# A mixture-of-experts gate matrix: one-hot products, or softmax weights scattered over zeros in DRAM

## The chip, the cores and the metric

The kernel runs on one core of one Trainium2 chip. The time is device microseconds of one execution. Five engines work side by side and meet at semaphores: TensorE (PE; its weight loads are listed as PEld), VectorE (DVE), ScalarE (ACT), GpSimd (POOL) and SyncE (SP). DMA transfers are issued from the queues of SP, ACT and POOL and share 16 DMA engines.

## The reference

Two transformer blocks on 512 tokens of width 1024. The change lies in the last part of the second block, a PEER layer with 8 heads and 128 x 128 = 16,384 experts:

```python
q = (xb @ w_query).reshape(T, 8, 2, 128)
s = einsum('thpk,hpnk->thpn', q, sub_keys)             # two lists of 128 scores per head
top_s, top_i = top_k(s, 16)
cand_s = top_s[:, :, 0, :, None] + top_s[:, :, 1, None, :]
cand_i = top_i[:, :, 0, :, None] * 128 + top_i[:, :, 1, None, :]
best_s, best_pos = top_k(cand_s.reshape(T, 8, 256), 16)
idx = take_along_axis(cand_i..., best_pos)             # 8 x 16 = 128 experts per token
gate = softmax(best_s)
act = gelu(einsum('td,thkd->thk', xb, expert_u[idx]))
out = einsum('thk,thkd->td', gate * act, expert_v[idx])
```

Each token has 128 picks, 16 in each of 8 heads. Two heads may pick the same expert; their gates then add.

## The kernel before, in words

**Weights in chunks.** Every weight matrix comes as chunks of 512 KB (128 rows of 1024 floats), 462 in all, through a ring of four buffers. SP issues the load (L687), ScalarE rounds to the high half WH (`split_high`, L261), VectorE subtracts for the low half WL (`split_low`, L267), and TensorE multiplies three times, high by high, high by low and low by high (`mm3`, L270 to L274). SP waits for the low half four chunks back, ScalarE for the multiplication four chunks back. So a chunk is split about three chunks ahead of its multiplication, and the three engines follow one order of chunks that is written out by hand.

**The peer_u stage.** 144 chunks, numbered p = 0 to 143: 16 query projections among the first 24, and 128 chunks of peer_u. For each of the latter TensorE makes one 128 x 512 block of x times u (128 experts by 512 tokens), ScalarE applies GELU (L1101) and SP stores it into the DRAM tensor `acts` (expert column, expert row, token). Beside them VectorE finds the picks, one tile of 128 tokens at a time: `pairs` (the best 16 of 256 sums, for two heads a call), `shifted`, `summed` (the numbers of the picks, found by comparing places that POOL subtracts at L795) and `listed` (the softmax). Calls of `low_of_next` stand between them, each one split; the tuples LOWS_LISTED and LOWS_SHIFTED say at which split each part ends, so that ScalarE and TensorE, in their own orders, take part at the same chunk.

**The gate matrix.** Tokens 0 to 383 (three tiles, DW = 384) are done densely: for them the kernel needs the gate of every expert. Before, TensorE transposes the lists of a tile (row number, column number, weight), ScalarE copies them (L1146), and from chunk 80 on 48 groups of 8 tokens follow (`before_gates`). For a group VectorE makes a 128 x 128 one-hot matrix of the row numbers for each token (L1707) and, with POOL's subtraction (L807), one of the column numbers times the weights (L1710); TensorE multiplies them, a float32 product of 128 x 128 per token (L2172, 16 instructions a group); ScalarE copies the result into a staging buffer (L1123) and after 8 groups writes 4 MB to the DRAM tensor `gate_matrices` (L1126).

**The v stage.** 128 chunks of peer_v, v = 0 to 127. For each, `weights(v)` on VectorE multiplies gates by acts (L1719), ScalarE rounds the product (L1135), VectorE makes its low half (L1723), and TensorE adds 18 products of 128 x 512 into PSUM, for three tiles. Gates and acts come in groups of four v, from DRAM, through a ring of two buffers (`load_group`, 768 KB and 768 KB, L1129 and L1130, issued from ScalarE's queue). The load of group j waits until VectorE has used the last weights of group j - 2. Gate reads are runs of 1 KB, act reads of 1.5 KB.

**The last tile.** Tokens 384 to 511 are done by gathering: for each of the 128 picks POOL gathers 128 rows of peer_v by indirect DMA (`pick_row`, L814, six buffers) and 128 acts of four bytes (`pick_acts`, L822), and VectorE adds row times weight into PSUM (`sum_row`, L1739), one per v. POOL starts them when the gate matrices have been written.

Of the kernel before, what the change touches and what calls it, by code (L numbers as in the profile page):

```python
# [13 lines left out]
F32 = mybir.dt.float32  # L14
F32R = mybir.dt.float32r
# [6 lines left out]
P = 128  # L22
# [23 lines left out]
NU = DW // 64  # L46
NG8 = 8 * NU
PICKS = PH * TOPK
SLOTS = 6
# [30 lines left out]
LOWS_LISTED = (47, 59, 71, 77)  # L80
LOWS_SHIFTED = (35, 47, 59, 71)


def before_gates(n):
    return 80 + 3 * n // 4

def constants():  # L90
# [27 lines left out]
    cols["token"] = (GT_TILE * P + i[:, None]).astype(f)  # L118
# [7 lines left out]
    for n, m in enumerate((64, 32, 16, 8, 4, 2, 1)):  # L126
# [7 lines left out]
              ("causal", P), ("cmp_ok", NT * 32), ("cmp_no", NT * 32), ("iota", P), ("four", 4), ("token", 1)]  # L134
# [12 lines left out]
def build(nc, d):  # L147
# [3 lines left out]
    with ExitStack() as ctx:  # L151
# [485 lines left out]
        LST = [A[:, 21504:21888], A[:, 21888:22272], XF[:, 0:384]]  # L637
        LST = [x.rearrange("p (l t) -> p l t", l=3) for x in LST]
        APART = XF[:, 2048:4096].rearrange("p (r i n) -> p r i n", r=2, i=8)
        zg, zs8 = misc(8), misc(8)  # L640

        HALF = 64
        STG = A[:, 0:16384].rearrange("p (r i t) -> p r i t", r=2, i=P)
        OHA = A[:, 16384:18432].rearrange("p (r n) -> p r n", r=16)
        OHB = A[:, 18432:20480].rearrange("p (r n) -> p r n", r=16)

        ACTED = [GATE[:, 0, 0:512], GATE[:, 0, 512:1024], ROW[:, 0:512], ROW[:, 512:1024]]
        G4 = A[:, 0:8 * DW].rearrange("p (r u i t) -> p r u i t", r=2, u=NU, i=4)
        AC = A[:, 8 * DW:16 * DW].rearrange("p (r i t) -> p r i t", r=2, i=4)
        WGHr = over("A", "WGH", 16 * DW, 4 * DW, F32R).rearrange("p (r t) -> p r t", r=4)  # L650
        WGLr = over("A", "WGL", 20 * DW, 4 * DW, F32R).rearrange("p (r t) -> p r t", r=4)
        WGH = WGHr.bitcast(F32)
        WF = A[:, 24 * DW:26 * DW].rearrange("p (r t) -> p r t", r=2)


        ROWS = A[:, 26 * DW:26 * DW + SLOTS * D].rearrange("p (r n) -> p r n", r=SLOTS)
        assert 26 * DW + SLOTS * D <= 16384
# [12 lines left out]
        acts_kept = nc.dram_tensor("acts", (P, P, S), F32, kind="Internal").ap()  # L670
        act_list = acts_kept.rearrange("e p (t o) -> (e p t) o", o=1)
# [75 lines left out]
        def _(pool):  # L747
# [35 lines left out]
            pool.dma_start(ROW[:, :], dr["nf_post"].partition_broadcast(P)).then_inc(sem("row_landed"), 16)  # L783
            pool.wait_ge(sem("rows_weighted"), 2 * NT)
# [5 lines left out]
            def places_apart(t, i):  # L790

                wait(pool, "eq_summed", 4 * t + i)
                p3 = PAB.rearrange("p s u -> p (s u)")[:, i * 64:i * 64 + 64].rearrange("p (h k) -> p h k", k=TOPK).unsqueeze(3)
                it = con("iota")[:, 0:TOPK].unsqueeze(1).unsqueeze(1)
                nc.gpsimd.tensor_tensor(EQ, p3.to_broadcast([P, PH // 2, TOPK, TOPK]),  # L795
                                        it.to_broadcast([P, PH // 2, TOPK, TOPK]), ALU.subtract).then_inc(sem("eq_ready"), 1)

            for t in range(NT):
                pool.wait_ge(sem("places_ready"), t + 1)
                for i in range(4):  # L800
                    places_apart(t, i)
            pool.wait_ge(sem("list_stored"), ND)
            pool.wait_ge(sem("picks_listed"), 1)
            for n in range(NG8):
                wait(pool, "onehot_ready", n - 1)
                nums = LST[n // 16][:, 1, 8 * (n % 16):8 * (n % 16) + 8].unsqueeze(2).to_broadcast([P, 8, P])
# [19 lines left out]
            for r in range(2):  # L826
                pool.wait_ge(sem(f"gates_written{r}"), 16 * NU // 2)
# [16 lines left out]
        def _(act):  # L844
# [268 lines left out]
            gm = dr["gate_matrices"]  # L1113

            def store_gates(n):
                u = n // 8
                if n % 8 == 0:
                    wait(act, f"gates_written{u % 2}", 16 * (u // 2))
                for b in (2 * n, 2 * n + 1):
                    act.wait_ge(sem("gm_ready"), b + 1)  # L1120
                    at = 4 * (b % 16)
                    dst = STG[:, u % 2].rearrange("p i t -> p t i")[:, at:at + 4, :]
                    nc.scalar.activation(dst, PS[:, b % 4, :].rearrange("p (t n) -> p t n", t=4), ACT.Copy)                        .then_inc(sem("gm_stored"), 1)  # L1123
                if n % 8 == 7:
                    act.wait_ge(sem("gm_stored"), 16 * (u + 1))
                    act.dma_start(gm[u], STG[:, u % 2]).then_inc(sem(f"gates_written{u % 2}"), 16)  # L1126
# [10 lines left out]
            for p in range(24, QU):  # L1137
                high_of_next()
                gelu(u_of(p))
                for t in range(NT):  # L1140
# [3 lines left out]
                    if t < ND and p == LOWS_LISTED[t] - 2:  # L1144
                        act.wait_ge(sem("list_turned"), t + 1)
                        nc.scalar.activation(LST[t], PS[:, 4, 0:3 * P].rearrange("p (l t) -> p l t", l=3), ACT.Copy)                            .then_inc(sem("list_stored"), 1)  # L1146
# [1127 lines left out]
```

## Time and profile before

| | us |
|---|---|
| median of 3 runs | 2643.19 (2641.51 to 2643.9) |
| the profiled execution | 2637.98 |
| its span on the core | 2636.1 |
| PE busy | 2519.1 (96%) |
| DVE busy | 1579.1 (60%) |
| ACT busy | 1027.7 (39%) |
| POOL busy | 502.8 (19%) |

Rows are read so. A group by line: line, engine, operation, out <- in with shapes, count | busy us, mean ns of one | idle time of the engine just before them, and what ended most of it. A window: its bounds and length, then busy us and count of PE, PEld, DVE, ACT and POOL, the granted clock of TensorE (1 is the full 2.4 GHz), the mean busy share of the DMA engines, GB/s. A timeline: start us, duration us, engine, line, operation, and in brackets the idle time before it. A piece of the chain: start, length, what. Matmuls are pipelined, so one of 0.39 us starts every 0.2267 us in a full stretch. A busy share of the DMA engines can come out slightly above 1.

### The profile page before, as it was taken

Reading aid. Unit: us, or ns where it says so; the run is one execution under the profiler, and the core shown is the slowest. Engines: PE = TensorE matmul, PEld = TensorE weight load, DVE = VectorE, ACT = ScalarE, POOL = GpSimd, SP = SyncE. Lnnn points to the kernel's source line nnn. Section 1 sums busy time; section 2 is a strip of 40 time slices with the busy share of each in tenths; the row PEclk is TensorE's granted clock in tenths of the full one; section 3 lists DMA queues with packets and bytes.
Section 4 is the critical chain, followed back from the end, with each engine's and each line's share of the span. In section 5 each row is a group of like instructions: output and inputs, shape, how many; then the busy total and the mean of one; then the engine's idle time right before and its main releaser. Section 6 shows DMA issues by size and latency. Waiting matters only on the chain.

```text
span 2636.1 us, 31762 instructions
## 1 busy us (share of the span) xinstructions
PE 2519.1 (96%) x11982; PEld 2081.6 (79%) x11982; DVE 1579.1 (60%) x2604; ACT 1027.7 (39%) x1452; POOL 502.8 (19%) x363
## 2 busy tenths in 40 slices
PE   7999998999999999899999999999999999899995
PEld 6876676888888788778888888888888778777784
DVE  4365665555543577467767755556322777777777
ACT  4353443433332644543333334555422333333332
POOL 0030000000000000000011123333100755566651
PEclk9997999999999999999999999999999999999998
DMA  6223343233322222133344443546645899889994
GB/s 207 82 67 97 94 137 99 85 98 99 97 96 96 80 80 72 57 117 104 122 146 144 144 144 139 205 160 229 236 146 190 308 329 334 310 320 320 316 336 145
DMA packets 162696, 434.03 MB, mean 165 GB/s; under 512 B 17072, under 2 KB 59072, under 8 KB 161280
## 3 DMA queue, kind: packets, MB, share of 16 engines
q1 hardware_dynamic: 94896, 276.96, 31.6%
q10 hardware_dynamic: 43424, 77.60, 8.4%
q0 software_dynamic: 24240, 77.63, 7.9%
q8 instruction: 89, 1.46, 0.2%
q14 instruction: 47, 0.39, 0.0%
HBM read 369.21 MB, written 62.91 MB: 164 GB/s over the span
## 4 chain that ended last, share of the span: by engine, by line
PE 71%; DVE 11%; DMA 8%; issue 4%; ACT 4%; POOL 1%; ACTq 0%; DVEq 0%; SPq 0%; POOLq 0%
PE PS L272 20%; PE PS L274 20%; PE PS L273 20%; DVE WL L267 4%; DMA A<-acts 4%; DMA A<-gate_matrices 3%; DVE PS L1739 3%; PE PS L2172 3%; DVE A L1719 2%; ACT WGH L1135 1%; PE PS L1935 1%; PE PS L2072 1%; PE PS L2019 1%; PE PS L2006 1%; POOL A L822 1%
## 5 line engine op out<-in xcount | busy, mean ns | idle before, releaser
L267 DVE TENSOR_TENSOR WL<-RAW,WH 128x1024 fp32r<-128x1024 f32 x462 | 587.1, 1272 | 557.9 <-ACT WH L261 520.6
L272 PE MATMUL PS<-HH,WH 128*128 128x512 f32 x1696 | 667.4, 394 | 8.8 <-DVE HL L433 7.1
L273 PE MATMUL PS<-HL,WH 128*128 128x512 f32 x1696 | 660.8, 390 | 0.0
L274 PE MATMUL PS<-HH,WL 128*128 128x512 f32 x1696 | 660.8, 390 | 0.0
L261 ACT ACTIVATE WH<-RAW 128x1024 fp32r<-128x1024 f32 x462 | 485.2, 1051 | 247.5 <-PE PS L274 209.6
L272 PEld LDWEIGHTS PS<-HH,WH 128*128 128x128 f32 x1696 | 318.8, 188 | 79.2 <-DVE HL L433 10.3
L274 PEld LDWEIGHTS PS<-HH,WL 128*128 128x128 f32 x1696 | 318.6, 188 | 66.6
L273 PEld LDWEIGHTS PS<-HL,WH 128*128 128x128 f32 x1696 | 318.9, 188 | 63.4
L272 PE MATMUL PS<-WH,WGH 128*128 128x512 f32 x768 | 307.2, 400 | 39.4 <-DVE WGL L1723 38.6
L273 PE MATMUL PS<-WL,WGH 128*128 128x512 f32 x768 | 304.8, 397 | 0.0
L274 PE MATMUL PS<-WH,WGL 128*128 128x512 f32 x768 | 304.4, 396 | 0.0
L814 POOL DMA_INDIRECT A<-in_peer_v,V_AT x128 | 187.9, 1468 | 225.7 <-DVE PS L1739 176.9
L272 PEld LDWEIGHTS PS<-WH,WGH 128*128 128x128 f32 x768 | 148.1, 193 | 75.4 <-issue 43.3
L1135 ACT ACTIVATE WGH<-A 128x384 fp32r<-128x384 f32 x128 | 67.2, 525 | 335.6 <-DVE A L1719 333.9
L273 PEld LDWEIGHTS PS<-WL,WGH 128*128 128x128 f32 x768 | 148.4, 193 | 30.9
L274 PEld LDWEIGHTS PS<-WH,WGL 128*128 128x128 f32 x768 | 147.8, 192 | 31.5
L1739 DVE SCALAR_TENSOR_TENSOR PS<-A,PS 128x1024 f32<-128x1024 f32 x127 | 163.0, 1283 | 2.1 <-DVE A L1732 0.6
L822 POOL DMA_INDIRECT A<-acts,A_AT x128 | 147.2, 1150 | 48.9 <-issue 38.7
L272 PE MATMUL PS<-WH,HH 128*128 128x512 f32 (+1 forms) x352 | 137.5, 391 | 12.5 <-DVE A L1554 5.5
L273 PE MATMUL PS<-WL,HH 128*128 128x512 f32 (+1 forms) x352 | 136.0, 386 | 0.0
L274 PE MATMUL PS<-WH,HL 128*128 128x512 f32 (+1 forms) x352 | 136.0, 386 | 0.0
L1101 ACT ACTIVATE ROW<-PS 128x512 f32<-128x512 f32 x64 | 38.3, 598 | 235.7 <-PE PS L274 235.7
(338 smaller groups left out, 3077.8 us busy)
## 6 DMA issues: line engine op xcount, KB each, us to landing
RAW<-in_peer_u SPq DMA_DIRECT2D x128, 512.0 KB, 3.5
RAW<-in_peer_v SPq DMA_DIRECT2D x128, 512.0 KB, 7.0
RAW<-in_w_ada SPq DMA_DIRECT2D x48, 512.0 KB, 3.7
gate_matrices<-A ACTq DMA_DIRECT2D x6, 4096.0 KB, 12.6
A<-gate_matrices ACTq DMA_DIRECT2D x32, 768.0 KB, 7.9
A<-acts ACTq DMA_DIRECT2D x32, 768.0 KB, 13.0
RAW<-in_ffn_up SPq DMA_DIRECT2D x44, 512.0 KB, 3.4
acts<-GATE SPq DMA_DIRECT2D x64, 256.0 KB, 2.3
```

Of the source, the lines that this page charges most:

```text
L261: nc.scalar.activation(WHr[:, slot(c), 0:w], RAW[:, slot(c), 0:w], ACT.Copy).then_inc(sem("high_done"), 1)
L267: nc.vector.tensor_tensor(WLr[:, slot(c), 0:w], RAW[:, slot(c), 0:w], WH[:, slot(c), 0:w], ALU.subtract).then_inc(sem("low_done"), 1)
L272: nc.tensor.matmul(out, L[0], R[0], start=first, stop=False)
L273: nc.tensor.matmul(out, L[0], R[1], start=False, stop=False)
L274: return nc.tensor.matmul(out, L[1], R[0], start=False, stop=last)
L814: pool.indirect_dma_start(out=ROWS[:, u % SLOTS, :], out_offset=None, in_=dr["peer_v"], in_offset=bass.IndirectOffsetOnAxis(ap=V_AT[:, u:u ...
L822: pool.indirect_dma_start(out=AG[:, u:u + 1], out_offset=None, in_=act_list, in_offset=bass.IndirectOffsetOnAxis(ap=A_AT[:, u:u + 1], axis ...
L1101: nc.scalar.activation(ACTED[k % 4], PS[:, 5 + k % 3, :], ACT.Gelu).then_inc(sem("gelu_done"), 1)
L1135: nc.scalar.activation(WGHr[:, v % 4, :], WF[:, v % 2, :], ACT.Copy).then_inc(sem("w_high"), 1)
L1719: nc.vector.tensor_tensor(WF[:, v % 2, :].rearrange("p (u t) -> p u t", u=NU), AC[:, j % 2, v % 4, :].rearrange("p (u t) -> p u t", u=NU), ...
L1739: ins = nc.vector.scalar_tensor_tensor(ACC, row, PW[:, u:u + 1], ACC, ALU.mult, ALU.add)
L2172: last = nc.tensor.matmul(PS[:, b % 4, j * P:(j + 1) * P], OHA[:, r, :], OHB[:, r, :], start=True, stop=True)
```

## The change

- The one-hot products go: POOL's subtractions, VectorE's two one-hot matrices a group, TensorE's products, the transposes of the lists, ScalarE's copies and the six writes of 4 MB.
- A DRAM tensor `gates` (129 x 128 x 384 floats: expert column, expert row, token) takes their place. POOL fills its first 128 slabs with zeros in 16 DMAs of 1.57 MB, one per two chunks of the up projection of the first block. VectorE waits for them before it overwrites the zeros' source, in the win2 stage.
- For each of the three dense tiles VectorE makes two lists of 128 numbers per token. `apart` compares each head's 16 experts with those of all heads before it, and sends a pick that came before to slab 128, which is never read. `merged` makes, for each pick, the sum of the weights of all picks with the same expert (128 instructions over 128 elements with an accumulated output). After every 16 a semaphore lets POOL go on.
- POOL scatters them: 3 x 128 indirect DMAs, each of which writes 128 floats, one per token.
- `summed` compares places itself on VectorE. `listed` of tile t is followed by `apart` and `merged` of tile t, no longer interleaved with the pairs of the next one. The splits stand at other places (LOWS_SHIFTED 35, 58, 81, 104).
- ScalarE waits at chunk 138 (QU - 6) for all scatters, where it waited for the writes of the gate matrices.
- The gate and act rings have three buffers in place of two, the row ring seven in place of six. The load of group j is issued at v = 4j - 11 (it was 4j - 6), when group j - 3 is used up. Gate reads are runs of 1.5 KB.
- POOL's first row picks wait for the picks' list and stand behind the scatters.

```diff
-SLOTS = 6
+SLOTS = 7
+GROUPS = 3
-LOWS_LISTED = (47, 59, 71, 77)
-LOWS_SHIFTED = (35, 47, 59, 71)
+LOWS_SHIFTED = (35, 58, 81, 104)
...
@@ POOL
+            nc.gpsimd.memset(ZERO, 0.0).then_inc(sem("zero_set"), 1)
+            for n in range(16):
+                pool.wait_ge(sem("chunk_used"), FIRST["up"] + 2 * n + 1)
+                pool.dma_start(gates_kept.rearrange("e p t -> p e t")[:, 8 * n:8 * n + 8, :],
+                               ZERO.unsqueeze(1).to_broadcast([P, 8, DW])).then_inc(sem("gates_zeroed"), 16)
...
-            for n in range(NG8):
-                nc.gpsimd.tensor_tensor(APART[:, n % 2], con("iota").unsqueeze(1).to_broadcast([P, 8, P]), nums,
-                                        ALU.subtract).then_inc(sem("rows_apart"), 1)
+            for t in range(ND):
+                for u in range(PICKS):
+                    if u % 16 == 0:
+                        pool.wait_ge(sem("picks_merged"), PH * t + u // 16 + 1)
+                    pool.indirect_dma_start(out=gate_list, out_offset=bass.IndirectOffsetOnAxis(ap=PLACE[:, t, u:u + 1], axis=0),
+                                            in_=MERGED[:, t, u:u + 1], in_offset=None).then_inc(sem(f"gates_placed{t}"), 16)
...
-            for r in range(2):
-                pool.wait_ge(sem(f"gates_written{r}"), 16 * NU // 2)
+            pool.wait_ge(sem("picks_listed"), 1)
             for u in range(SLOTS):
                 pick_row(u)
@@ ScalarE
                 if p == QU - 6:
-                    for r in range(2):
-                        act.wait_ge(sem(f"gates_written{r}"), 16 * NU // 2)
+                    for t in range(ND):
+                        act.wait_ge(sem(f"gates_placed{t}"), 16 * PICKS)
...
-                    for j in range(2):
+                    for j in range(GROUPS):
                         load_group(j)
...
-                if v % 4 == 2 and 2 <= v // 4 + 2 < P // 4:
+                if v % 4 == 1 and v // 4 + GROUPS < P // 4:
@@ VectorE
+            def apart(t):
+                places = []
+                nc.vector.memset(TIMES[:, 0:TOPK], 0.0)
+                for h in range(1, PH):
...
+                    done = mark(nc.vector.tensor_tensor(same, EXPERT[:, hs].unsqueeze(2).to_broadcast([P, TOPK, n]),
+                                                        EXPERT[:, 0:n].unsqueeze(1).to_broadcast([P, TOPK, n]), ALU.is_equal))
+                    until(done)
+                    places.append(mark(nc.vector.tensor_reduce(TIMES[:, hs], same, AX, ALU.add)))
+                    low_of_next(h in (3, 5, 7))
...
+            def merged(t, b):
+                for u in range(16 * b, 16 * b + 16):
+                    last = nc.vector.scalar_tensor_tensor(SAME[:, u % 16, :], EXPERT, EXPERT[:, u:u + 1], GW, ALU.is_equal,
+                                                          ALU.mult, accum_out=MERGED[:, t, u:u + 1])
+                last.then_inc(sem("picks_merged"), 1)
+                dve.wait_ge(sem("picks_merged"), PH * t + b + 1)
...
+            for t in range(NT):
                 for i in range(4):
                     low_of_next()
+                    last = pairs(t, i)
+                    low_of_next()
+                until(last)
+                shifted(t)
+                for i in range(4):
+                    low_of_next()
+                    summed(t, i)
+                listed(t)
+                if t < ND:
+                    apart(t)
+                    for b in range(PH):
                         low_of_next()
+                        merged(t, b)
@@ TensorE
-            def gates_of(n):
-                pe.wait_ge(sem("onehot_ready"), n + 1)
-                for b in (2 * n, 2 * n + 1):
-                    wait(pe, "gm_stored", b - 3)
-                    for j in range(4):
-                        r = 8 * (n % 2) + 4 * (b % 2) + j
-                        last = nc.tensor.matmul(PS[:, b % 4, j * P:(j + 1) * P], OHA[:, r, :], OHB[:, r, :],
-                                                start=True, stop=True)
-                    last.then_inc(sem("gm_ready"), 1)
```

## Rows read from the trace of the kernel before

**Rows 1.** The page, busy time of the engines

```profile
PE 2519.1 (96%) x11982; PEld 2081.6 (79%) x11982; DVE 1579.1 (60%) x2604; ACT 1027.7 (39%) x1452; POOL 502.8 (19%) x363
```

**Rows 2.** Windows: up projection; one-hot products; v stage; two short stretches of it

```profile
510.00:760.00 250.00, 250.00 (x1105) 207.01 (x1104) 138.24 (x163) 89.45 (x119) 0.00 (x0) 1.00 0.30 97
1604.00:1883.00 279.00, 279.00 (x1603) 244.75 (x1603) 161.11 (x127) 145.24 (x167) 89.47 (x44) 1.00 0.49 182
...
2035.00:2616.00 581.00, 541.48 (x2304) 442.98 (x2304) 435.56 (x524) 193.98 (x255) 329.75 (x252) 0.96 0.88 309
...
2200.00:2210.00 10.00, 10.00 (x46) 8.29 (x45) 5.39 (x6) 1.97 (x3) 5.63 (x5) 1.00 1.04 398
...
2282.00:2286.00 4.00, 1.25 (x3) 1.09 (x4) 2.32 (x3) 1.51 (x2) 2.87 (x3) 0.51 0.27 62
```

**Rows 3.** Groups by line, of TensorE, VectorE and POOL in the v stage

```profile
L272 PE MATMUL PS<-WH,WGH 128*128 128x512 f32 x768 | 307.2, 400 | 39.4 <-DVE WGL L1723 38.6 <-ACT ROW L1101 0.7
...
L1719 DVE TENSOR_TENSOR A<-A 128x384 f32<-128x384 f32 x128 | 70.7, 552 | 54.3 <-issue 46.1 <-DMA A<-acts 8.1
...
L822 POOL DMA_INDIRECT A<-acts,A_AT x128 | 147.2, 1150 | 48.9 <-issue 38.7
```

**Rows 4.** ScalarE's timeline: GELU of chunks 24, 25 and 143

```profile
1299.92 0.60 ACT L1101 ACTIVATE GATE<-PS 128x512 f32<-128x512 f32 x1 [4.88 <-PE PS L274]
...
1305.36 0.60 ACT L1101 ACTIVATE GATE<-PS 128x512 f32<-128x512 f32 x1 [3.89 <-PE PS L274]
...
2034.61 0.60 ACT L1101 ACTIVATE ROW<-PS 128x512 f32<-128x512 f32 x1 [3.48 <-PE PS L274]
```

**Rows 5.** The chain, first and last of the twelve long pieces of L2172

```profile
1600.18 3.57 PE PS L2172 x32
...
1858.75 3.57 PE PS L2172 x32
```

**Rows 6.** DMA issues: KB each, us to landing; the act loads' own view

```profile
RAW<-in_ffn_up SPq DMA_DIRECT2D x44, 512.0 KB, 3.4
...
L1130 ACTq DMA_DIRECT2D A<-acts x32: 567/568/1710, 2008.0 to 2575.4; - x32
...
DMA to landing us min/median/max: 6.6/13.0/23.8
```

**Rows 7.** VectorE's timeline: a call of `pairs`, a split, `summed`, part of `listed`

```profile
1389.68 0.75 DVE L1620 TENSOR_TENSOR X<-X 128x256 f32<-128x256 f32 x2
...
1394.04 1.20 DVE L267 TENSOR_TENSOR WL<-RAW,WH 128x1024 fp32r<-128x1024 f32 x1
1395.16 1.42 DVE L1646 SCALAR_TENSOR_TENSOR A<-A,X 128x256 f32<-128x256 f32 x4
1396.62 1.22 DVE L1649 TENSOR_REDUCE X<-A 128x64 f32<-128x1024 f32 x1
...
1401.12 0.29 DVE L1659 TENSOR_TENSOR X<-X,MISC 128x128 f32<-128x128 f32 x1
```

**Rows 8.** Groups by line: ScalarE's reads of its accumulator

```profile
L921 ACT ACTIVATION_READ_ACCUMULATOR A<-PS,MISC 128x1 f32 x64 | 12.4, 194 | 0.0
```

**Rows 9.** Timelines of POOL and VectorE in the v stage; landing times of L822

```profile
2137.00 0.95 POOL L822 DMA_INDIRECT A<-acts,A_AT  x1 [0.30 <-issue]
...
2143.02 1.28 DVE L1739 SCALAR_TENSOR_TENSOR PS<-A,PS 128x1024 f32<-128x1024 f32 x1
...
2143.26 0.95 POOL L822 DMA_INDIRECT A<-acts,A_AT  x1 [0.30 <-issue]
...
2049.42 0.56 DVE L1723 TENSOR_TENSOR WGL<-A,WGH 128x384 fp32r<-128x384 f32 x1 [0.59 <-ACT WGH L1135]
2049.50 1.30 POOL L822 DMA_INDIRECT A<-acts,A_AT  x1 [0.30 <-issue]
...
2440.01 1.68 POOL L814 DMA_INDIRECT A<-in_peer_v,V_AT  x1 [2.26 <-DVE PS L1739]
...
DMA to landing us min/median/max: 2.3/5.0/8.1
```

More of the change, by code:

```diff
@@ new lines, in build @@
+        WGH = WGHr.bitcast(F32)
+        WF = A[:, o4 + 2 * GD:o4 + 2 * GD + 2 * DW].rearrange("p (r t) -> p r t", r=2)
+        o5 = o4 + 2 * GD + 2 * DW
+        ROWS = A[:, o5:o5 + SLOTS * D].rearrange("p (r n) -> p r n", r=SLOTS)
+        SAME = A[:, o5:o5 + 2048].rearrange("p (r n) -> p r n", r=16)
+        SAME2 = A[:, o5 + 2048:o5 + 4096].rearrange("p (r n) -> p r n", r=16)
+        TIMES, PLACED = A[:, 21248:21376], A[:, 21376:21504]
+        assert 11264 <= o5 and o5 + SLOTS * D <= 20480
@@ L658, in build @@
+        PLACE = over("A", "PLACE", 21504, ND * PICKS, U32).rearrange("p (t u) -> p t u", t=ND)
+        MERGED = A[:, 21888:22272].rearrange("p (t u) -> p t u", t=ND)
+        ZERO = A[:, 21504:21504 + DW]
         ACC = PS[:, 2 * GT_TILE:2 * GT_TILE + 2, :]
@@ L1641, in summed @@
             def summed(t, i):
-                dve.wait_ge(sem("eq_ready"), 4 * t + i + 1)
+                places = PAB.rearrange("p s u -> p (s u)")[:, i * 64:i * 64 + 64].rearrange("p (h k) -> p h k", k=TOPK)
+                ranks = con("iota")[:, 0:TOPK].unsqueeze(1).unsqueeze(1)
+                link(nc.vector.tensor_tensor(EQ, places.unsqueeze(3).to_broadcast([P, PH // 2, TOPK, TOPK]),
+                                             ranks.to_broadcast([P, PH // 2, TOPK, TOPK]), ALU.is_equal))
@@ L1644, in summed @@
                 for h in range(PH // 2):
                     num = TFf[:, i * 64 + 16 * h:i * 64 + 16 * h + TOPK].unsqueeze(1).to_broadcast([P, TOPK, TOPK])
[L1646 to L1650 removed]
+                    last = nc.vector.tensor_tensor(EQ[:, h], EQ[:, h], num, ALU.mult)
@@ L2178, in _ @@
                 acts(u_of(p))
-                for t in range(NT):
-                    if t < ND and p == LOWS_LISTED[t] - 2:
-                        pe.wait_ge(sem("list_ready"), t + 1)
-                        wait(pe, "list_stored", t)
-                        for l, src in enumerate((N12[:, t % 2, 0], N12[:, t % 2, 1], BV[:, t % 2].rearrange("p h k -> p (h k)"))):
-                            last = nc.tensor.transpose(PS[:, 4, l * P:(l + 1) * P], src, ident)
-                        last.then_inc(sem("list_turned"), 1)
-                for n in range(NG8):
-                    if before_gates(n) == p + 1:
-                        gates_of(n)
             pe.wait_ge(sem("gelu_done"), P)
```

154 lines of the change are left out of this document (46 added, 108 removed).

## The prediction

> **What bounds the kernel now.** I read the page first. TensorE is busy for 96% of the span [rows 1], so the first question of every edit is whether it takes TensorE work away or makes TensorE wait. Then the windows by stage, which show three states [rows 2]. In the up projection and in the stage with the one-hot products TensorE is busy all the time at granted clock 1.00. In the last stage (the 128 chunks of peer_v, here "the v stage") it is busy 541.5 of 581 us at clock 0.96, and the DMA share is 0.88. Third, the groups by line [rows 3]: in the v stage TensorE sat idle 39.4 us, nearly all of it behind the weights L1723, and VectorE 54.3 us before L1719, the line that waits for the gate and act groups. Fourth, ScalarE's timeline in the peer_u stage, which gives the pace: one chunk per 5.44 us, with the GELU of chunk 24 ending at 1300.5 and that of the last, chunk 143, at 2035.2 [rows 4]. 119 chunks x 5.44 would end at 1947.9, so 87.3 us is something else. The chain shows what: twelve pieces of 32 instructions of L2172, the one-hot products, of 3.57 us each [rows 5]. They are half of its 768, the rest stands in shorter pieces between; 24 x 3.57 = 85.7 us. Three sets of transposes make up the rest. TensorE never waits there for anything but its own work.
>
> **The change, part by part.**
> *One-hot products and transposes out.* They are wholly on TensorE's path: -87.3 us. The ScalarE copies, the six 4 MB writes, POOL's subtractions and VectorE's one-hot rows that fed them ran beside TensorE and give nothing themselves.
>
> *Zeros.* 16 writes of 1.57 MB (25.2 MB) over some 32 chunks of the up stage add about 145 GB/s to 97 [rows 2]; the same table has 398 GB/s in one stretch. A weight chunk lands in 3.4 us [rows 6] and is asked for about two chunks (10.9 us) ahead; one zero block at 398 GB/s is 4.0 us, so even right behind one it comes at 7.4 us. Cost 0; if that cover fails, up to 16 x 4 us.
>
> *VectorE's new list work.* A tile now has 23 chunks, 23 x 5.44 = 125 us. In it: 23 splits at 1.2 = 28; four pairs of searches at 4.35 (1389.68 to 1394.04 [rows 7]) = 17; the place comparison (about 1.2), four products (1.42) and the sum (1.22) four times = 15; the comparisons of `apart`, 7,168 elements and as many summed, at 1.22 us per 1,024 elements = 17; small steps 4; and 128 instructions of `merged`. Their duration is not in the trace. Lower bound: the pitch of a 128-wide operation, 0.21 us (0.29 long [rows 7], of which some 0.08 overlaps the next). Upper: that plus 0.19, what ScalarE's accumulator read takes [rows 8]. So 27 to 51 us, 108 to 132 in all for 125. I take 0.29 (37 us): VectorE keeps up. At the upper end it is late by 7 us per tile against a lead of nearly three chunks, about 10 us of waits at most, and those lie ahead of the wait below and come off it. Price 0.
>
> *The scatter, on POOL.* 384 indirect DMAs in a row, and nothing else passes it: the row picks queue behind it. The nearest rows are L822's gathers, 128 four-byte elements each [rows 3, 9]. With VectorE idle one takes 0.95 us plus 0.30 between (2137.0), also beside an operation with one of its inputs in PSUM (2143.3); one that starts inside an operation with two inputs in SBUF waits for its end and takes 1.30 (2049.5). The mean over the v stage is 1.15 + 0.30 = 1.45. Here the splits occupy 1.2 of 5.44 us: 0.22 x half of 1.2 = 0.13 us each; the list work by the same sum adds 0.14. So 1.53 us while VectorE builds lists, 1.39 later. Start: split L becomes possible some 1 us (the high half) after the GELU of chunk L - 4, at 1301.5 + 5.44 (L - 28) [rows 4]; the first `merged` block stands behind split 42, 1377.7, and the long comparisons before it put it some 11 us behind: 1389. VectorE's lists end near split 108, 1737: 348 us, 228 scatters. The other 156 take 217 us: 1954, and 5.0 us to land [rows 9]: 1959.
> ScalarE asks for all of them after the GELU of chunk 138, at 1920.7, and nothing passes it. Queued behind: the first group loads and the high halves of chunks 142 and on. TensorE can go on to the end of 141 (1937). Restart: six issues at up to 0.57 [rows 6], 3 us, high and low half 2.3, chunks 142 and 143 10.9: the v stage begins at 1975 in place of 1947.9. After a gap TensorE also runs slowly at first: granted clock 0.51, the lower level of 1.2 GHz, in 2282 to 2286 [rows 2], when it had just stood idle. All gaps of the v stage cost 541.5 - 522 = 19 us that way, about 2 each. Together +29. Bounds: 1.26 us per scatter, no wait, 0; 1.68 + 0.30 as L814 after a wait [rows 9], the slow rival below.
> The SBUF — State Buffer page of the Trainium skill ("Who interferes with whom") says of `tensor_tensor` that it was not seen to stall DMA, since descriptor generation needs the write side only. The trace differs here: 1.30 against 0.95 beside exactly such an operation. By that rule each scatter would be 1.26 us and the wait would be nothing.
>
> *Deeper rings, longer gate rows.* 2,304 matmuls at 5.44/24 = 0.2267 us are 522 us, the stage, whose window [rows 2] holds them all, lasts 580: 58 us of late groups and slow restarts. A group is asked for when its buffer is free, four v before its use, 16 us, and the act loads take 6.6 to 23.8 us to land [rows 6]. With three buffers the lead is eight v, 33 us, more than the longest. What is late next is DMA itself: share 0.88 x 580/522 = 0.98, rate 309 x 580/522 = 343 GB/s, against 1.04 and 398 in a full stretch [rows 2]. That leaves few per cent, so not all comes back. Gate reads of 1.5 KB runs in place of 1 KB help a little. Bounds 0 and 58; I take 46, nearer the upper since the longest landing fits. A seventh row buffer: 0, rows aren't waited for now. The end after the last matmul is as before.
>
> **Sum** against the profiled execution, 2638.0: -87.3 +29 -46 = 2533.7. The median of the runs shown is 5.2 us over that execution, so 2539.
>
> **Rivals.**
> 1. *The scatter hides.* At up to about 1.37 us each it is done by 1915 and landed by 1920: 2510. For: 0.95 + 0.30 whenever VectorE is idle. Against: the 1.45 mean. 20%.
> 2. *The DMA engines are the bound of the v stage.* The groups still come late, since 0.98 of share is no reserve, and the 46 stay out: 2585. For: full stretches already occur. Against: there are nearly idle ones too, around each stall (share 0.27 in 2282 to 2286 [rows 2]). 20%.
> 3. *Slower: a scatter costs more than a gather.* Place: POOL, between chunk 39 and the wait at 138. Each 0.1 us over 1.53 moves the end by 38 us one for one. All gains are gone when the v stage begins at 2035 + 46 = 2081, that is (2081 - 21 - 1389)/384 = 1.75 us each. At 1.98, L814's rate after a wait, scatters end at 2149, the v stage starts at 2171 and the time is about 2734. For: no row shows a four-byte write to DRAM; an engine's eight writes may not overlap. Against: the gathers of the same shape do. 12%.
> The DMA: Bandwidth & Descriptors page of the Trainium skill (Specifications) speaks for it: under 512 bytes a transfer becomes a read-modify-write. No run here shows that yet.
> 4. *The lists make VectorE late*, `merged` at over 0.4 us: TensorE waits in each of three tiles, and the wait at 138 shrinks by as much; some 2550. 5%.
> The rest, 43%, is the forecast. The change does take the products out, so a change that does nothing is not a rival.
>
> **How the numbers follow.** 2539 is the likeliest case. The low end, 2495, is rival 1 with the whole 58 us; the high end, 2610, lies past rival 2 and holds scatters up to about 1.63 us with the 46 regained. Left out are most of rival 3 and a mix of 1 with more. A measurement of this kernel tells about 0.2%, 5 us, from no change. Faster: the forecast, rivals 1, 2 and 4, less 2 for places where two go wrong together = 0.86. Of those 2 and rival 3's 12, 11 are slower and 3 the same.
>
> **What would show it.** Right: no L2172; GELU every 5.44 us up to chunk 138; then one gap of TensorE of 20 to 35 us whose releaser is the landing of a scatter; POOL busy without a break from about 1390 to 1950, 1.4 to 1.5 us per scatter; in the v stage VectorE's idle time before `weights` at a fifth of 54 us and DMA share 0.95 or more. Wrong: a gap over 100 us (rival 3), none (1), a v stage still near 580 us (2), or TensorE waiting for low halves between chunks 39 and 100 (4).

## The result: 2896 us, slower by 9.3%, and the profile after

| | before | after |
|---|---|---|
| median of the runs | 2643.6 us (4 runs) | 2895.6 us (4 runs) |
| ratio, 95% interval | | 1.0932 (1.0882 to 1.0983) |
| profiled execution, span | 2638.0, 2636.1 | 2898.4, 2896.4 |
| last GELU ends | 2035.2 [rows 4] | 2348.6 |
| v stage | about 580 [rows 2] | 527 |

One of the four executions after, 2926.8 us, ran in the chip's slower state and is left out of the ratio.

The forecast was 2539 us and faster. The page of the changed kernel: busy time, the granted clock and the DMA share in 40 slices, the chain by engine, and four groups.

```profile
PE 2495.2 (86%) x11205; PEld 2005.5 (69%) x11205; DVE 1638.4 (57%) x3352; ACT 939.7 (32%) x1353; POOL 769.9 (27%) x700
...
PEclk9997999999999999999757955985599999999998
DMA  5322432664322213234203410330154479999994
...
PE 82%; issue 12%; DVE 3%; ACT 2%; DMA 1%; POOL 0%; DVEq 0%; SPq 0%; ACTq 0%
...
L264 PE MATMUL PS<-HH,WH 128*128 128x512 f32 x1696 | 681.6, 402 | 108.8 <-issue 99.1
...
L796 POOL DMA_INDIRECT gates<-A,PLACE x384 | 391.1, 1019 | 547.6 <-DVE A L1662 412.1
...
L1662 DVE SCALAR_TENSOR_TENSOR A<-A 128x128 f32<-128x128 f32 x384 | 114.4, 349 | 71.0 <-issue 70.7
```

TensorE has 777 matmuls fewer than before [rows 1] and yet ends later. The clock falls three times in the middle, the DMA share with it, and 12% of the chain is "issue": time in which an engine waits for nothing that the profile shows. The scatter itself is cheap for POOL: 1.02 us each. The three falls begin some 20 us after POOL starts a burst of scatters; the windows below show them.

The windows of the changed kernel (columns: stretch, its length, then for PE, PEld, DVE, ACT and POOL the busy us with the count of instructions, the granted clock, the DMA share and GB/s): three stretches in which scatters are issued, one between them without scatters, the v stage.

```profile
1388.00:1540.00 152.00, 56.59 (x159) 34.26 (x158) 44.99 (x231) 7.72 (x10) 112.50 (x112) 0.59 0.14 35
...
1640.00:1810.00 170.00, 64.53 (x176) 39.28 (x175) 48.05 (x244) 9.26 (x12) 127.88 (x128) 0.58 0.13 36
...
1904.00:2064.00 160.00, 69.09 (x189) 42.33 (x188) 48.72 (x251) 10.81 (x14) 121.31 (x119) 0.61 0.15 43
...
1574.00:1636.00 62.00, 62.00 (x275) 51.33 (x274) 53.84 (x101) 21.04 (x27) 0.00 (x0) 1.00 0.41 131
...
2349.00:2876.00 527.00, 523.01 (x2304) 431.83 (x2302) 438.56 (x524) 198.84 (x254) 327.16 (x250) 1.00 0.93 337
```

Without scatters TensorE runs 275 matmuls in 62 us, 4.44 per us. In the first three rows it ran 524 in 482 us; at 4.44 per us they take 118, so 364 us were lost there. What that looks like from inside, in the timeline of all engines (start, duration, engine, instruction, and the idle time before it):

```profile
1449.77 0.97 POOL L796 DMA_INDIRECT gates<-A,PLACE  x1 [0.31 <-issue]
1449.79 0.58 PE L265 MATMUL PS<-HL,WH 128*128 128x512 f32 x1 [2.22 <-issue]
1451.04 0.97 POOL L796 DMA_INDIRECT gates<-A,PLACE  x1 [0.30 <-issue]
1451.18 0.29 PEld L266 LDWEIGHTS PS<-HH,WL 128*128 128x128 f32 x1 [2.51 <-issue]
...
1452.58 0.59 PE L266 MATMUL PS<-HH,WL 128*128 128x512 f32 x1 [2.20 <-issue]
...
1453.98 0.29 PEld L264 LDWEIGHTS PS<-HH,WH 128*128 128x128 f32 x1 [2.51 <-issue]
...
1455.37 0.35 DVE L1662 SCALAR_TENSOR_TENSOR A<-A 128x128 f32<-128x128 f32 x1 [1.31 <-issue]
```

A matmul, a weight load, a matmul, a weight load start at 1449.79, 1451.18, 1452.58 and 1453.98: one instruction of TensorE every 1.40 us, none of which waits for a semaphore. VectorE has such gaps too, if less evenly: most of its instructions in `merged` start 1.40 us apart between 1455 and 1473, but four of them in the same stretch came at their usual 0.27 (1452.34 to 1453.15). POOL keeps its pace of 0.97 + 0.30. The low clock is not the cause: the matmul takes 0.58 us at it, in place of 0.39, but the next starts 2.8 us later. And the DMA engines are not full: their share is 0.14. SP issued 5 weight loads in the 140 us from 1400, where 26 go in a kernel that is not held.

The harm has an onset. These are windows before it, at it and behind it (the count of POOL is that of the scatters):

```profile
1380.00:1400.00 20.00, 20.00 (x90) 16.57 (x89) 19.79 (x106) 5.14 (x7) 9.24 (x9) 1.00 0.56 159
1400.00:1420.00 20.00, 16.25 (x59) 10.84 (x58) 11.74 (x66) 1.96 (x3) 15.62 (x15) 0.90 0.30 80
...
1460.00:1480.00 20.00, 4.11 (x7) 2.00 (x7) 3.17 (x15) 1.54 (x2) 15.42 (x16) 0.50 0.06 14
```

Up to 1410 TensorE runs at full pace beside the scatters. Its first gap comes when 16 of them have started, while the clock is still high; in the other two bursts it comes after about as many. Behind the onset TensorE runs 7 matmuls in 20 us in place of 90. The end of the third burst shows the same with VectorE idle (9 matmuls from 2050 to 2076), so its lists need not run beside the scatters to keep TensorE slow.

The v stage went nearly as forecast: its DMA share is 0.93, where 0.95 or more was expected, and VectorE's idle time before `weights` is gone. The group of L264 there has 4.7 us of idle time in place of 39.4 [rows 3]:

```profile
L264 PE MATMUL PS<-WH,WGH 128*128 128x512 f32 x768 | 299.2, 390 | 4.7 <-DVE WGL L1705 4.0 <-ACT ROW L1088 0.7
```

### The profile page after: what moved, and what is told of

Its sections match the earlier page's. It is cut to its first block, busy times and chain, and to the rows that moved or that the text cites. A ratio compares the mean times of both kernels' runs of the same rounds, so it can differ in the third digit from the quotient of the medians.

```text
span 2896.4 us, 31168 instructions
## 1 busy us (share of the span) xinstructions
PE 2495.2 (86%) x11205; PEld 2005.5 (69%) x11205; DVE 1638.4 (57%) x3352; ACT 939.7 (32%) x1353; POOL 769.9 (27%) x700
## 4 chain that ended last, share of the span: by engine, by line
PE 82%; issue 12%; DVE 3%; ACT 2%; DMA 1%; POOL 0%; DVEq 0%; SPq 0%; ACTq 0%
PE PS L264 25%; PE PS L266 24%; PE PS L265 24%; PE PS L1913 1%; PE PS L2050 1%; PE PS L1997 1%; PE PS L1984 1%; DVE WL L259 1%; PE PS L408 1%; PE PS L2128 0%; PE PS L414 0%; DMA RAW<-in_w_in 0%; ACT WH L253 0%; ACT A L444 0%; PE PS L1916 0%
## 5 line engine op out<-in xcount | busy, mean ns | idle before, releaser
L259 DVE TENSOR_TENSOR WL<-RAW,WH 128x1024 fp32r<-128x1024 f32 x462 | 564.4, 1222 | 712.0 <-ACT WH L253 611.7
L264 PE MATMUL PS<-HH,WH 128*128 128x512 f32 x1696 | 681.6, 402 | 108.8 <-issue 99.1
L265 PE MATMUL PS<-HL,WH 128*128 128x512 f32 x1696 | 677.8, 400 | 110.0 <-issue 109.4
L266 PE MATMUL PS<-HH,WL 128*128 128x512 f32 x1696 | 678.1, 400 | 108.9 <-issue 108.2
L796 POOL DMA_INDIRECT gates<-A,PLACE x384 | 391.1, 1019 | 547.6 <-DVE A L1662 412.1
L264 PEld LDWEIGHTS PS<-HH,WH 128*128 128x128 f32 x1696 | 327.1, 193 | 200.8 <-issue 127.2
L266 PEld LDWEIGHTS PS<-HH,WL 128*128 128x128 f32 x1696 | 327.0, 193 | 200.7 <-issue 136.8
L265 PEld LDWEIGHTS PS<-HL,WH 128*128 128x128 f32 x1696 | 327.3, 193 | 189.8 <-issue 127.5
L264 PE MATMUL PS<-WH,WGH 128*128 128x512 f32 x768 | 299.2, 390 | 4.7 <-DVE WGL L1705 4.0
L1088 ACT ACTIVATE GATE<-PS 128x512 f32<-128x512 f32 x64 | 38.3, 598 | 455.0 <-PE PS L266 215.2
L264 PEld LDWEIGHTS PS<-WH,WGH 128*128 128x128 f32 x768 | 144.1, 188 | 36.1 <-issue 5.2
L1662 DVE SCALAR_TENSOR_TENSOR A<-A 128x128 f32<-128x128 f32 x384 | 114.4, 349 | 71.0 <-issue 70.7
L264 PE MATMUL PS<-WH,HH 128*128 128x512 f32 (+1 forms) x352 | 137.6, 391 | 12.6 <-DVE A L1524 5.5
```

What stands on the lines that cost most here:

```text
L259: nc.vector.tensor_tensor(WLr[:, slot(c), 0:w], RAW[:, slot(c), 0:w], WH[:, slot(c), 0:w], ALU.subtract).then_inc(sem("low_done"), 1)
L264: nc.tensor.matmul(out, L[0], R[0], start=first, stop=False)
L265: nc.tensor.matmul(out, L[0], R[1], start=False, stop=False)
L266: return nc.tensor.matmul(out, L[1], R[0], start=False, stop=last)
L796: pool.indirect_dma_start(out=gate_list, out_offset=bass.IndirectOffsetOnAxis(ap=PLACE[:, t, u:u + 1], axis=0), in_=MERGED[:, t, u:u + 1], ...
L1088: nc.scalar.activation(ACTED[k % 4], PS[:, 5 + k % 3, :], ACT.Gelu).then_inc(sem("gelu_done"), 1)
```

## The experiments

Each starts from the changed kernel unless its diff says otherwise. Where no ratio stands, the time is that of one execution.

### The scatters away, and the deeper rings alone

```diff
# e1: no scatter, no wait for it
-  pool.indirect_dma_start(out=gate_list, out_offset=...PLACE[:, t, u:u + 1]..., in_=MERGED[:, t, u:u + 1], ...)
-  for t in range(ND):
-      act.wait_ge(sem(f"gates_placed{t}"), 16 * PICKS)
# e4: the kernel before, with
-SLOTS = 6
+SLOTS = 7
+GROUPS = 3      # G4 and AC have GROUPS buffers, the loads run GROUPS groups ahead
```

> The changed kernel without its 384 scatters and without ScalarE's wait for them; the merged weights are computed and thrown away, the gate matrix in DRAM stays zero. In the changed kernel the GELU chunks kept a pitch of 5.44 us outside three stretches and 16 to 67 us in them, some 400 us more than their number by 5.44. Theory A (those stretches belong to the scatters, nothing else of the change costs anything): 2897 less 400 is 2497 us; between 2485 and 2515, TensorE's clock above 0.95 from 1388 to 1950 us, last GELU near 1950 us. Theory B (the longer lists of VectorE, or the splits of the gates put ahead, hold TensorE in these stretches): 2800 to 2900 us, the stretches remain.

> The kernel before with the deeper rings alone (three groups of gates and activations on one semaphore each, seven row slots), one-hot products kept. Theory A (the rings are worth the 54 us that the v stage of the changed kernel got shorter, 526 against 580 us): 2643 less 50 is about 2593 us, between 2583 and 2605. Rival (the shorter v stage belongs to what the change removed, not to the rings): 2635 to 2645 us.

Measured: e1 2501.5 us (ratio to before 0.9466, 0.9439 to 0.9494), e4 2588.7 us (0.9801, 0.9779 to 0.9822). Their windows, e1's first burst stretch and v stage, then e4's v stage:

```profile
1380.00:1560.00 180.00, 180.00 (x795) 149.07 (x794) 169.01 (x685) 53.92 (x69) 0.00 (x0) 1.00 0.47 144
...
1950.00:2476.00 526.00, 521.69 (x2298) 431.23 (x2299) 438.10 (x524) 199.17 (x254) 329.80 (x251) 1.00 0.93 337
```

```profile
2038.00:2564.00 526.00, 520.90 (x2289) 430.35 (x2288) 434.94 (x521) 195.34 (x251) 331.15 (x250) 1.00 0.94 336
```

VectorE does all its list work in e1 and TensorE never stops in the stretch: the lists are innocent. The rings are worth 2641.7 - 2588.7 = 53 us (2641.7 is the kernel before, measured beside them), and what the change adds to them without the scatter is worth 2588.7 - 2501.5 = 87.2 us. The loss belongs to the scatters.

### Which property of a scatter does it

Twelve kernels vary three quantities: how many bytes each of the 128 writes has, how far apart they go, and whether in order; the direction (e2) and the kind of transfer (f4) come beside them. The edits, in the line that makes the places and in the transfer:

```diff
-  nc.vector.scalar_tensor_tensor(PLACE[:, t], PLACED, float(DW), token, ALU.mult, ALU.add)
+  # in floats, u the pick, p the partition, t the tile, n1 the first key of the pick
+  # f1: 16384 t + 128 u + p               f2, e3, f3: 128 (16384 t + 128 u + p)
+  # g1, h1, i2: 49152 p + 384 u + 128 t   h2: 49152 u + 384 p + 128 t
+  # g2: 384 (128 u + n1) + 128 t + p      h3: 128 (16384 t + 128 u + n1) + p
# e2: a gather from the changed kernel's own places (slab 128 is zeroed too; the third tile waits for the first)
-  pool.indirect_dma_start(out=gate_list, out_offset=..., in_=MERGED[:, t, u:u + 1], in_offset=None)
+  pool.indirect_dma_start(out=SINK[:, ...], out_offset=None, in_=gate_list, in_offset=...)
# e3, h1: rows of 512 bytes; f3, i2: of 64 bytes
+  pool.indirect_dma_start(out=row_list, out_offset=..., in_=con("mean")[:, 0:128 or 0:16], in_offset=None)
# f4: an ordinary transfer
+  pool.dma_start(gates_kept[u, :, P * t:P * t + 1], MERGED[:, t, u:u + 1])
```

> Every scatter becomes an indirect gather of 128 x 4 bytes from the very same addresses of the gate matrix into a buffer that nobody reads; the matrix stays zero, and one more row of it is zeroed. As many instructions on GpSimd, as many descriptors, the other direction. Theory W (it is the 4-byte writes to DRAM that slow the other engines): about 2497 to 2520 us, no stretch in which TensorE's instructions come 1.4 us apart. Theory I (it is the dense run of indirect transfers with their descriptors, whichever way the data goes): about 2900 us, the three stretches as before.

> Every scatter writes 128 rows of 512 bytes (a constant of the program in place of the weights) to 128 neighbouring rows of the gate matrix, in order; the output is not the reference's. As many transfers and descriptors, 128 times the bytes (25 MB in all, at 1.28 us for 64 KB some 51 GB/s while they run). Theory W with the size as its cause (writes under 512 bytes cost a read as well): the slow stretches are gone, 2500 to 2560 us. Theory I (the run of indirect transfers): stretches as before, 2880 to 3000 us.

> The changed kernel's scatters, 4 bytes from each partition as before, but to 128 neighbouring floats of DRAM (512 bytes in all) in place of 128 far apart ones; the places are now in order, so the output is not the reference's. Theory S (the number of 4-byte writes counts, wherever they go): three slow stretches as in the changed kernel, 2880 to 2900 us. Theory R (it is the far addresses, each write opening another part of the memory): 2525 us like the run with 512-byte rows. Between them, if neighbours collide in one 512-byte line and each must wait for the other: longer than the changed kernel.

> The same 4-byte scatters at a pitch of 512 bytes, in order: the first 4 bytes of each of the rows that the run with 512-byte rows wrote whole; the output is not the reference's. This and that run differ in the size of the write alone. Theory S (small size): 2880 to 2900 us with the three stretches. Theory R (addresses without order): 2525 us.

> The same addresses at a pitch of 512 bytes, each row 64 bytes long (a constant in place of the weights). Theory S as a threshold at 512 bytes (each shorter write costs a read and a write back): 2880 to 2900 us. Rival (only writes shorter than some smaller piece are slow): 2525 us.

> 384 ordinary transfers from GpSimd in place of the indirect ones, each 4 bytes from each partition to fixed places 1536 bytes apart; the output is not the reference's. Theory S (the 4-byte writes, whoever makes their descriptors): the three stretches stay, 2860 to 2950 us. Rival (small writes and indirect descriptors only together, for instance through the writing of the list of places by GpSimd): about 2525 us.

| run | each write | places of one scatter | us | 1400 to 1540: matmuls, clock, DMA share |
|---|---|---|---|---|
| e2 | gather, 4 bytes | the changed kernel's own | 2525.1 | 620, 1.00, 0.47 |
| e3 | 512 bytes | 64 KB in order | 2527.1 | 620, 1.00, 0.60 |
| f3 | 64 bytes | 64 KB in order | 2526.8 | 619, 1.00, 0.49 |
| f2 | 4 bytes | 64 KB in order | 2530.1 | 619, 1.00, 0.48 |
| f1 | 4 bytes | 512 bytes in order | 2566.9 | 611, 1.00, 0.91 |
| f4 | 4 bytes, ordinary | 192 KB in order | 2498.1 | 619, 1.00, 0.51 |

Each of these times stands on one execution. The faster kernels that were executed four times spread over 5 to 12 us (e4, i1, e1), so differences under some 12 us between rows are not read here.

So it is not the run of indirect transfers (e2, e3), and my theory S, that the small size is enough, fell with f2, f3 and f4: none of them holds the engines. f1 shows a different cost. The windows of f2 and then f1:

```profile
1400.00:1540.00 140.00, 140.00 (x619) 115.95 (x619) 129.77 (x497) 43.10 (x55) 110.42 (x98) 1.00 0.48 146
```

```profile
1400.00:1540.00 140.00, 138.48 (x611) 114.35 (x610) 125.40 (x470) 42.52 (x52) 110.72 (x97) 1.00 0.91 133
...
RAW<-in_peer_u SPq DMA_DIRECT2D x25, 512.0 KB, 17.5
```

With 128 neighbouring floats the DMA engines are busy for 0.91 of the time at 133 GB/s and a 512 KB weight load takes 17.5 us to land, but TensorE goes on. It costs 37 us more than f2. Of f4 one thing more: it started 39 transfers of 4-byte writes in the 20 us from 1400, where the change started 15, and TensorE kept its pace. The places remained:

> Every scatter writes its 128 x 4 bytes 192 KB apart, one in each of 128 equal parts of the matrix, in order; the next scatter writes 1536 bytes further on. The output is not the reference's. At a pitch of 512 bytes (64 KB in one scatter) there was no slow stretch; the changed kernel's own places lie anywhere in 25 MB. Theory F (what costs is how far the 4-byte writes of one scatter lie apart): the three stretches are back, 2800 to 2950 us. Theory U (what costs is that the places have no order): about 2530 us.

> The places keep the drawn first key of each pick and lose the second: the 128 x 4 bytes of scatter u lie without order, at 128 rows of 1536 bytes drawn by the picks, in a window of 192 KB that moves on with u; the output is not the reference's. Theory F (distance): no slow stretch, about 2530 us. Theory U (no order): the stretches as in the changed kernel, 2880 us or more.

> The run with 4 bytes every 192 KB (2901 us) with whole 512-byte rows at the same starts, a constant in place of the weights; 25 MB are written. Theory D (many distant places in one scatter are slow, whatever the size): 2850 to 2950 us and the three stretches. Theory M (distance and small size together: a short write to a distant place): 2525 to 2540 us as with 512-byte rows in order.

> Indirect scatters of 4 bytes at a pitch of 1540 bytes in order, 192 KB in each scatter: the window of the run with drawn first keys (2915 us), without its disorder and without two writes in one row; and about the places of the ordinary transfers (2498 us) by indirect ones. Theory O (within 192 KB disorder or rows hit twice are what costs): 2525 to 2535 us. Theory D (a scatter that leaves 64 KB is slow, if its places come by a list): 2880 to 2920 us.

> Indirect scatters of 4 bytes within 64 KB, as in the run with a pitch of 512 bytes in order (2530 us), but each in the row of 512 bytes that the first key of its pick draws: disorder, and rows hit by several partitions. Theory O (disorder or rows hit twice): 2880 us or more. Theory D (distance, pages of 64 KB or the like): 2530 us.

> Rows of 64 bytes, a constant in place of the weights, at the 192 KB pitch at which 4 bytes took 2901 us and 512 bytes 2527. Theory M512 (every write under 512 bytes to a distant place is slow): 2880 to 2920 us. Rival (64 bytes are whole pieces for the memory; only smaller writes are slow): 2527 us.

| run | each write | places of one scatter | us | 1400 to 1540: matmuls, clock, DMA share |
|---|---|---|---|---|
| g1 | 4 bytes | 192 KB apart, in order | 2901.2 | 136, 0.59, 0.12 |
| i2 | 64 bytes | 192 KB apart, in order | 2529.7 | 619, 1.00, 0.50 |
| h1 | 512 bytes | 192 KB apart, in order | 2527.2 | 619, 1.00, 0.60 |
| g2 | 4 bytes | within 192 KB, rows drawn | 2914.9 | 134, 0.57, 0.13 |
| h2 | 4 bytes | within 192 KB, in order | 2531.9 | 620, 1.00, 0.49 |
| h3 | 4 bytes | within 64 KB, rows drawn | 2530.4 | 619, 1.00, 0.48 |

The windows of g1 and h1, which differ in the size of the write alone:

```profile
1400.00:1540.00 140.00, 51.90 (x136) 29.84 (x135) 39.72 (x194) 6.18 (x8) 107.00 (x107) 0.59 0.12 34
```

```profile
1400.00:1540.00 140.00, 140.00 (x619) 115.95 (x618) 129.71 (x491) 42.44 (x55) 110.41 (x98) 1.00 0.60 190
```

Both conditions are needed: 4-byte writes, and places that are scattered widely. Either alone is harmless: 64 and 512 bytes at the widest pitch (i2, h1), 4 bytes within 64 KB or in order within 192 KB (f2, h3, h2). The longer writes were tried in order only, not at drawn places. Theory M had h1 right; its strict form, with a limit at 512 bytes, fell with i2. Theories O and D were each half right: disorder costs in 192 KB and not in 64 KB, distance costs in order too (g1). In g2 and h3 several writes of a scatter can also fall into one row; g2 doesn't tell that from disorder. What unit of distance stands behind this (64 KB is the widest that was harmless without order) is not settled. The places of h2 are 1536 bytes apart by its edit (its expectation says 1540), the same as those of f4. The changed kernel meets both conditions, as its picks are drawn from 16,384 experts in 25 MB.

### How many in flight

```diff
   pool.indirect_dma_start(... MERGED[:, t, u:u + 1] ...)
+  # g3, h4, i1, j1: wait until all but 0, 1, 2 or 3 of the scatters so far have landed
+  # (a semaphore for each scatter in flight)
```

> GpSimd waits for each scatter to land before it makes the next, at most one in flight; all places are the changed kernel's own. Landing takes 2 to 3 us in a quiet stretch, so a scatter each 3.5 to 5 us in place of 1.28. Theory Q (what holds the engines is a queue of unfinished writes, which the rate builds up: the first 12 scatters cost nothing): no slow stretch; but GpSimd needs 384 x 4 = 1540 us, ends near 2930 us, the v stage waits for it, some 3450 us. Rival (each scatter costs the other engines a fixed time, about 1.06 us of TensorE each, whatever the rate): TensorE's clock stays low from 1388 us on, and its instructions are spread out through the whole stretch.

> The changed kernel's own places, at most two scatters in flight. One at a time took 2.87 us for each from 1393 to 2496 us and showed no slow stretch in its first 140 us. With two, 1.6 to 2.0 us for each. Theory Q (a queue that fills above some rate, between one scatter per 1.28 us and one per 2.9 us, and holds the engines only when full): no stretch of slow engines, the scatters end between 2110 and 2180 us, the v stage starts then: 2660 to 2760 us. Rival (each scatter has a fixed price for the engines, which one at a time pays as well): the price per scatter is that of the changed kernel, 1.06 us, and TensorE's clock is low through the stretches, 2900 us.

> The changed kernel with its own places, at most three scatters in flight; the output is whole. Two in flight took 2.39 us for each in the first burst, landing 3.7 us, 1.87 in the second and 1.28 in the third, and held no engine; unlimited scatters that cost nothing (rows of 512 bytes) came every 1.50, 1.47 and 1.37 us and ended at 1944. Theory Q (a queue of unfinished short writes fills only above a number in flight): three in flight give some 1.65, 1.5 and 1.37 us each, the last near 1975, the v stage starts some 30 us later than with 512-byte rows: 2545 to 2580 us, which would beat both kernels. Rival (the rate decides, and near 1.5 us for each the queue fills as before): slow stretches return, TensorE's clock under 0.9 in them, 2750 to 2900 us.

> As with three in flight (2563 us, last scatter at 1979), with at most four; the output is whole. Theory Q (a limit by the number in flight, above four): scatters come at the pace of those that cost nothing (1.50, 1.47, 1.37 us), the last near 1950, 2530 to 2550 us. Rival (the limit lies between three and four, or the rate decides): the slow stretches are back at least in part, over 2600 us, TensorE's clock below 0.95 in 1400 to 1540.

| at most in flight | us | last scatter starts | 1.40 us stretches |
|---|---|---|---|
| 1 (g3) | 3078.5 | 2496.3 | none |
| 2 (h4) | 2685.4 | 2102.5 | none |
| 3 (i1) | 2563.3, ratio to before 0.9721 (0.9675 to 0.9767) | 1978.8 | none |
| 4 (j1) | 2901.3, ratio 1.0964 (1.0928 to 1.0999) | 2078.8 | all three |
| no limit (the change) | 2895.6 | 2075.0 | all three |

The windows of i1, then of j1:

```profile
1388.00:1540.00 152.00, 152.00 (x672) 125.91 (x671) 141.56 (x562) 46.19 (x59) 104.81 (x90) 1.00 0.48 146
...
1640.00:1810.00 170.00, 170.00 (x752) 140.85 (x751) 103.95 (x360) 52.01 (x67) 118.69 (x111) 1.00 0.48 152
```

```profile
1388.00:1540.00 152.00, 64.17 (x201) 43.41 (x200) 55.09 (x266) 12.36 (x16) 105.59 (x106) 0.62 0.17 46
...
1640.00:1810.00 170.00, 62.66 (x179) 38.81 (x177) 52.80 (x263) 10.01 (x13) 120.32 (x120) 0.59 0.14 40
```

Three are harmless, four are as bad as no limit. The waits of POOL say how small the step is; i1, then j1 (waited for: us in total, times, longest):

```profile
POOL gates L796 <- issue: 94.2, 296, 2.2
POOL gates L796 <- DMA gates<-A,PLACE: 79.1, 87, 2.8
```

```profile
POOL gates L796 <- issue: 115.1, 377, 0.4
...
POOL gates L796 <- DMA gates<-A,PLACE: 0.5, 1, 0.5
```

With three allowed POOL was stopped 87 times, 79 us in all. With four it was stopped once, for 0.5 us; so at this pace, which is the change's own, more than four are hardly ever in flight as the semaphores count it, and the change's slow stretches don't need more. So my picture of a long queue that fills (theory Q) fails as a count of scatters that have not landed: between harmless and ruinous lies one more. Something builds up all the same, since the first 16 to 19 scatters of a burst cost nothing in the change, in g1, in g2 and in j1. Whether that is writes for which the semaphore has already been raised, no run here shows.

The limit also lowers the rate, and the two were not varied apart: beside VectorE's lists i1 starts a scatter per 1.69 and 1.53 us (90 in 152 us, 111 in 170), j1 one per 1.43 and 1.42. That the rate decides alone is unlikely, though. From 1826 to 1900 i1 started 53 in 74 us, one per 1.40, and TensorE ran 328 matmuls there, as many as in the same window of the change, where no scatter was under way; j1 fell into its first slow stretch after 16 that came 1.38 us apart. In i1's timeline of POOL in that window the pitch is for most scatters the change's own 1.28 us:

```profile
1850.83 0.97 POOL L796 DMA_INDIRECT gates<-A,PLACE  x1 [0.30 <-issue]
1852.11 0.97 POOL L796 DMA_INDIRECT gates<-A,PLACE  x1 [0.30 <-issue]
1853.50 0.97 POOL L796 DMA_INDIRECT gates<-A,PLACE  x1 [0.43 <-DMA gates<-A,PLACE]
```

i1 is the fastest kernel that computes the whole output. One semaphore wait in POOL's loop turns 2896 into 2563 us. What it still pays is the end of the scatters: the last start of h1 is 1944.2, of i1 1978.8, and those 34.6 us are nearly all of the 36 us between 2527.2 and 2563.3.

## Why the prediction was wrong

**One-hot products out -87.3, zeros 0, VectorE's lists 0: right together.** e1 differs from e4 in all three, and takes 87.2 us less. They weren't measured one by one, so a gain and a loss among them could cancel. `merged` takes 0.35 us with 0.08 for its read beside it, at a pitch of 0.27 where nothing disturbs it; I had taken 0.29.

**Deeper rings, -46: right, a little small.** -53 by e4, and the v stage is 526 us. What I held back, that a share of 0.98 leaves no reserve, wasn't needed: e4 and e1 ran the stage at a DMA share of 0.93 and 0.94 and the clock at 1.00. Rival 2 is out.

**The scatter's own path, +29: right in its total where the writes are harmless, and partly by luck.** In e3 it is 2527.1 - 2501.5 = 25.6, with one gap of 27.2 us, forecast at 20 to 35, and the last GELU ends at 1977.3, forecast 1975. But two terms were off and cancel. The scatters start at 1390.9 and 1944.1, first and last, 1.44 us each, where I had 1.53 and 1.39; the last is out 10 us early, and ScalarE goes on at 1946.5, not 1959. Then its six group loads take 14.3 us to issue, where I had 3: the last alone holds ScalarE for 10.67 us (3.31 us in e1). e3's source view of the scatter, then rows of its timelines of ScalarE and TensorE:

```profile
L797 POOL DMA_INDIRECT gates<-CON,PLACE x384: 965/972/3762, 1390.9 to 1944.1; - x192
...
1946.46 0.40 ACTq L1103 DMA_DIRECT2D A<-gates  x1
...
1950.10 10.67 ACTq L1105 DMA_DIRECT2D A<-acts  x1
...
1963.33 0.76 PE L264 MATMUL PS<-HH,WH 128*128 128x512 f32 x1 [27.20 <-DVE WL L259]
...
1976.65 0.60 ACT L1089 ACTIVATE ROW<-PS 128x512 f32<-128x512 f32 x1 [3.48 <-PE PS L266]
```

The forecast's own terms against the median of before measured beside e1, 2641.7 - 87.3 - 46 + 29, give 2537; the kernels with the same number of harmless indirect transfers (f1 aside) take 2525 to 2532.

**The step that failed.** It is "the nearest rows are L822's gathers", from which the scatter was priced as time of POOL and of the wait at chunk 138 alone. A bound was kept for a dearer scatter (rival 3, 1.98 us each, 2734), but on POOL's account. The real price is on everybody else's: POOL paid 1.02 + 0.30 us per scatter, less than forecast, while TensorE, from some 20 us after the start of each burst to its end, got one instruction per 1.40 us, and VectorE 99 in the 120 us from 1420, where i1 has 374. That is 2898 - 2527 = 371 us against the harmless scatters of e3. So rival 3 had the sign and the missing row ("no row shows a four-byte write to DRAM") and the wrong mechanism: its gap at 138 is not there, and the gap's reason, late scatters, isn't either: the last scatter starts at 2075.0, the first group load behind chunk 138 at 2321.1. The gathers of the same shape and the same addresses (e2) prove nothing about scatters.

**Two slips in the forecast's arithmetic**, which decide nothing: its mean was (1954 - 1389)/384 = 1.47 us per scatter, so rival 3's "each 0.1 us over 1.53" holds over 1.47; and rival 1 with the whole 58 us gives 2498, not 2495.

**The rule of the Trainium skill** that I set beside rival 3 (DMA: Bandwidth & Descriptors, Specifications: under 512 bytes a transfer becomes a read-modify-write) names the right thing to fear, small writes. As a limit at 512 bytes these runs don't bear it out in time: 64-byte writes, near (2526.8) or far (2529.7), cost what 512-byte ones do (2527.1 and 2527.2), and 4-byte ones within 64 KB can't be told from them (2530.1 and 2530.4). Whether a read-modify-write stands behind the slow case no run here shows.

## What stays open

Through what these writes hold the instructions of TensorE and VectorE. The trace records no waiting for it. All runs here carry the profile's records, so whether those records take part in the jam wasn't tried; if they do, a run without them would lose less. Number in flight and rate were not varied apart, and nothing between 4 and 64 bytes was tried. Of the kernels of the two tables each was executed once; the harmless ones, without f1 and f4, agree within 7 us and lie some 370 us below g1 and g2.

## What to carry to other kernels

Before one product of TensorE's is exchanged for many tiny writes to DRAM, price the writes on the other engines too, and measure the scatter by itself in the real places: a gather, an ordered pattern or a longer row at the same rate may say nothing about it. If "issue" gaps of one constant length appear on several engines at once while the DMA share is low, look for who writes small pieces far apart, and bound how many are in flight: here a limit of three gave 2563 us, four gave 2901. Since that edge is narrow, the deeper rings alone (2589 us, ratio 0.9801, 95% interval 0.9779 to 0.9822) are the safer part of this change, and a change made of several parts should be tried part by part.

## What was not expected of the hardware

- 384 scatters of 128 x 4 bytes to places spread over 192 KB or more without order, or 192 KB apart, cut TensorE from 4.44 matmuls per us to 7 in 20 us, from about the 17th scatter of a burst to its end. Whoever looks at averages sees only a low clock and a low DMA share.
- The step between harmless and ruinous is one more scatter allowed in flight, three to four.
- Scatters into 128 neighbouring floats do another harm: a DMA share of 0.91 at 133 GB/s, and weight loads that land in 17.5 us.
- An ordinary transfer of 128 x 4 bytes costs POOL less than an indirect one: f4 started 158 in the 140 us in which f2 started some 98, and its last one started at 1713.9, so nothing waited for it at chunk 138 (2498.1 us in all).
